# Row loads after the mixture of experts split over three queues, and attention outputs copied by ScalarE alone

## The reference

```python
for i in range(2):
    h += mixer_i(rmsnorm(h))        # layer 0: latent attention with a paged cache; layer 1: chunked gMLP gating
    h += hier_moe(rmsnorm(h))       # 4 groups x 8 experts, the 2 best of one group per token
    h += sigmoid(rmsnorm(h) @ ple_w_gate) * (p_i @ ple_w_proj)
y = rmsnorm(h)

# the end of the attention
o = einsum('bshc,chv->bshv', o_lat, w_uv)      # 8 heads, 256 latent -> 128
mix = o.reshape(...) @ w_o

# hier_moe: gates is zero except at the token's two experts
a = silu(t @ w_gate[e]) * (t @ w_up[e]) * gates[:, e]
y = sum over e of a @ w_down[e]
```

## Time and profile before

| | us |
|---|---|
| runs shown | 1202.03, 1206.19, 1210.29 |
| profiled execution, its own time | 1208.84 |
| its span | 1207.1 |
| PE busy | 1090.9 (90% of the span) |
| DVE busy | 362.3 (30%) |
| ACT busy | 194.0 (16%) |
| POOL busy | 115.3 (10%) |
| chain that ended last | PE 67%, DMA 22%, DVE 4%, issue 3% |
| row loads, POOL's queue | 8 of 512 KB (median 6.0 us from issue to landing), 4 of 128 KB (6.9 us) |
| weight stream, SP's queue | 250 of 1024 KB (18.7 us) |

### The profile page before, as it was taken

How to read it: one execution, slowest core, us unless ns; L and a number is a source line. 1 busy time by engine, 2 the same in 40 slices (tenths; PEclk the granted TensorE clock), 3 DMA queues, 4 the chain that set the end, 5 groups by cost and what they waited for, 6 DMA issues and landing times.

```text
span 1207.1 us, 14547 instructions
## 1 busy us (share of the span) xinstructions
PE 1090.9 (90%) x5302; PEld 667.0 (55%) x5302; DVE 362.3 (30%) x909; ACT 194.0 (16%) x398; POOL 115.3 (10%) x152
## 2 busy tenths in 40 slices
PE   5898879999998888899999999999999998887793
PEld 4675547644443333577777777777654443332372
DVE  1233432432221211353225544420332222210164
ACT  2121211311111111222111211000121111111121
POOL 0124200011111110100000000000011111110101
PEclk9898989989999999999999999999989999999996
DMA  9727727269999999783333433334349999999521
GB/s 384 263 75 225 224 90 309 79 250 403 419 419 419 419 419 376 304 361 110 135 128 117 140 105 105 105 128 139 108 155 396 419 417 418 419 419 422 204 102 40
DMA packets 62597, 306.81 MB, mean 254 GB/s; under 512 B 13730, under 2 KB 23170, under 8 KB 30402
## 3 DMA queue, kind: packets, MB, share of 16 engines
q1 hardware_dynamic: 45936, 276.52, 58.1%
q0 software_dynamic: 13632, 22.58, 5.8%
q10 hardware_dynamic: 2962, 6.80, 1.5%
HBM read 308.88 MB, written 21.08 MB: 273 GB/s over the span
## 4 chain that ended last, share of the span: by engine, by line
PE 67%; DMA 22%; DVE 4%; issue 3%; ACT 1%; SPq 0%; ACTq 0%; POOL 0%; POOLq 0%; DVEq 0%
DMA ring_sb<-stream 22%; PE ps L1558 16%; PE ps L1413 11%; PE ps L1606 8%; PE ps L1422 4%; PE ps L1491 3%; PE ps L1328 3%; PE ps L1143 2%; PE ps L1163 2%; PE ps L1371 2%; PE ps L1131 2%; PE ps L1362 1%; PE ps L1509 1%; PE ps L1507 1%; PE ps L1236 1%
## 5 line engine op out<-in xcount | busy, mean ns | idle before, releaser
L1413 PE MATMUL ps<-ring_sb,scr_sb 128*64 128x512 f32 x1024 | 238.3, 613 | 39.4 <-DMA ring_sb<-stream 39.4
L1558 PE MATMUL ps<-hn_sb,ring_sb 128*128 128x288 f32 x768 | 195.0, 408 | 0.0
L1413 PEld LDWEIGHTS ps<-ring_sb,scr_sb 128*64 128x64 f32 x1024 | 79.3, 140 | 193.2 <-issue 193.1
L1558 PEld LDWEIGHTS ps<-hn_sb,ring_sb 128*128 128x128 f32 x768 | 142.6, 190 | 37.3 <-DVE hn_sb L715 0.3
L1422 PE MATMUL ps<-ring_sb,scr_sb 128*64 128x512 f32 x512 | 123.7, 628 | 2.1 <-ACT scr_sb L602 1.9
L950 DVE SCALAR_TENSOR_TENSOR scr_sb<-ps,scr_sb 128x256 f32<-128x256 f32 x32 | 15.5, 484 | 266.9 <-ACT scr_sb L598 266.9
L1606 PE MATMUL ps<-scr_sb,ring_sb 128*128 128x288 f32 x384 | 95.3, 407 | 0.0
L1606 PEld LDWEIGHTS ps<-scr_sb,ring_sb 128*128 128x128 f32 x384 | 72.2, 190 | 19.4
L1422 PEld LDWEIGHTS ps<-ring_sb,scr_sb 128*64 128x64 f32 x512 | 35.5, 142 | 63.7 <-issue 60.0
L1491 PE MATMUL ps<-scr_sb,ring_sb 128*128 128x288 f32 x256 | 64.3, 406 | 0.0
L345 POOL DMA_INDIRECT scr_sb<-hn_rows,scr_sb x32 | 32.5, 1017 | 299.9 <-DVE scr_sb L927 275.1
(11 more groups left out here) (251 smaller groups left out, 1119.0 us busy)
## 6 DMA issues: line engine op xcount, KB each, us to landing
ring_sb<-stream SPq DMA_DIRECT2D x250, 1024.0 KB, 18.7
scr_sb<-key_pages SPq DMA_DIRECT2D x64, 192.0 KB, 3.4
ring_sb<-row_pages POOLq DMA_DIRECT2D x64, 128.0 KB, 3.2
scr_sb<-y_rows POOLq DMA_DIRECT2D x8, 512.0 KB, 6.0
hn_rows<-scr_sb ACTq DMA_DIRECT2D x4, 512.0 KB, 3.8
h_sb<-x SPq DMA_DIRECT2D x1, 1152.0 KB, 5.5
scr_sb<-bs ACTq DMA_DIRECT2D x1, 640.0 KB, 13.4
scr_sb<-p ACTq DMA_DIRECT2D x2, 288.0 KB, 5.2
```

What stands on the lines that cost most here:

```text
L1413: last = mm(ps[64 * a:64 * a + 64, 2 + b, :], xT[:, k, 64 * a:64 * a + 64], slot(a + 2 * (k // 4))[:, (k % 4) * 512:(k % 4) * 512 + 512], ...
L1558: last = mm(bank((i + 1) % 4, T), ring(s, (i % 2) * D + k * P, P), hn_t[:, k, :], start=(k == 0), stop=(k == KD - 1))
```

## The change

Two edits. The six row loads are shared out by token tile: tile 0 by SP, tile 1 by ACT, tile 2 by POOL. POOL raises a new semaphore `rows_put` where it used to issue all six; SP and ACT wait for it. SP's two loads stand just ahead of the waits that it had already. ACT's two stand behind its branch and ahead of its table load. And all eight heads are copied by ACT, with one semaphore `o_sb` in place of `o_a` and `o_d`; DVE only waits for the last head's matmuls.

```diff
+    def load_rows(engine, L, t):
+        t0, tn = TOK[t]
+        for k in range(2):
+            engine.dma_start(y12[0:tn, k, t, :], y_rows[L][k * T + t0:k * T + t0 + tn, :]
+                             ).then_inc(sem(f"y12_in{t}"), 16)
...
             if s == S_GATE[0]:
+                sp.wait_ge(sem("rows_put"), 1)
+                load_rows(sp, 0, 0)
                 sp.wait_ge(sem("y12_in1"), 32)
                 sp.wait_ge(sem("y12_in2"), 32)
...
             if s == S_GATE[1]:
+                sp.wait_ge(sem("rows_put"), 2)
+                load_rows(sp, 1, 0)
                 sp.wait_ge(sem("y12_in1"), 64)
                 sp.wait_ge(sem("y12_in2"), 64)
...
-            for t, (t0, tn) in enumerate(TOK):
-                for k in range(2):
-                    pool.dma_start(y12[0:tn, k, t, :], y_rows[L][k * T + t0:k * T + t0 + tn, :]
-                                   ).then_inc(sem(f"y12_in{t}"), 16)
+            pool.sem_inc(sem("rows_put"), 1)
+            load_rows(pool, L, 2)
...
-        for h in range(0, H, 2):
+        for h in range(H):
             act.wait_ge(sem("o_ps"), h + 1)
-            nc.scalar.activation(oT[:, h, :], bank(h % 4, T), ACT.Copy).then_inc(sem("o_a"), 1)
+            nc.scalar.activation(oT[:, h, :], bank(h % 4, T), ACT.Copy).then_inc(sem("o_sb"), 1)
...
+            act.wait_ge(sem("rows_put"), L + 1)
+            load_rows(act, L, 1)
             nc.scalar.activation(eps[:, 2:3], eps[:, 0:1], ACT.Sqrt)
...
-        for h in range(1, H, 2):
-            dve.wait_ge(sem("o_ps"), h + 1)
-            nc.vector.tensor_copy(oT[:, h, :], bank(h % 4, T)).then_inc(sem("o_d"), 1)
+        dve.wait_ge(sem("o_ps"), H)
...
-                pe.wait_ge(sem("o_a" if h % 2 == 0 else "o_d"), (h - 4) // 2 + 1)
+                pe.wait_ge(sem("o_sb"), h - 3)
...
-        pe.wait_ge(sem("o_a"), H // 2)
-        pe.wait_ge(sem("o_d"), H // 2)
+        pe.wait_ge(sem("o_sb"), H)
```

## The result

The changed kernel took 1210.6 us (median of 20 runs, 1204.53 to 1219.3); the kernel before, beside it, 1204.15 us. The ratio is 1.0045, 95% interval 1.0027 to 1.0063: **0.45% slower, 5.4 us by the ratio**. The medians themselves lie 6.5 us apart. The forecast was 0.26% slower, 1209.3 us. The sign, the place and the mechanism were right, the size came out larger.

The account below looks back on a forecast made before the run. PE and what it waits for were taken to bound the kernel. Late tile 1 rows (1.6 + 1.5 us) less 0.05 for the last head copy gave 1206.2 + 3.1 = 1209.3 us; range (1206 - 3) to 1216.

Parts of the forecast that it names:

- What bounds it; the margins: Before the combination: PE sets the end, without waiting for row loads, which land 1.6 and 1.3 us ahead of it.
- Tile 0 to SP, tile 2 on POOL: nothing: Row loads of tiles 0 and 2: both hidden, tile 0 in 6 us ahead of PE; cost and gain 0.
- Tile 1: time of issue: ACT's row loads, behind its last copy and branch: first issue at 495.11 in layer 0, 1140.47 in layer 1.
- Rival 1: Nothing is late: ACT's sequencer runs ahead and issues from 494.2; 0.1 us a layer, 1206.4 us; chance 0.22.
- Tile 1: time to land: ACT's row loads: 4.9 and 4.8 us from first issue, so 1.6 and 1.5 us late for PE's combination.
- What is late next: First gate slot and spatial weights after the combination: slot's margin 0.5 to 0.6 us, weights' 1.4 us; taken at 0.
- ACT's table load and first square: ACT behind its two row-load issues: table load ends at 497.3, covered by the first square at about 501.9; 0.
- The head copies: All eight on ACT: it keeps up, only the last copy is on the path, a gain of 0.05 us.
- Rival 2: PE's clock falls at the combination or an ACT issue is slow: up to 1216.8 us; chance 0.13.
- Rival 3: Faster: row loads before the change land later in other executions, so PE waits; 1.1 us at most, 1205.1; chance 0.05.
- The sum: Whole kernel: 1.6 + 1.5 - 0.05 = +3.1 us, 1209.3 us on the median, 0.26% slower.
- The promise of the change: Parallel issue of the six row loads: POOL's issues take 3.19 us, their landing is hidden, so no gain.

Follow-up runs that it names:

- the kernel with one filler: The kernel before with 1 keep-busy matmul instead of 3 in front of the combination: 1207.39 us, ratio 1.0017.
- the kernel with four large loads on SP: The changed kernel with tile 1 loaded by SP behind tile 0, instead of by ACT: 1209.17 us, ratio 1.0016.
- the rows alone: The changed kernel with the head copies given back to DVE, so only the row loads moved: 1211.27 us, ratio 1.0058.

## Why the prediction was right, and where its size was off

- **What bounds it; the margins.** Right for the trace that it read: PE did not wait, and the margins were 1.6 and 1.3 us, as the kernel with one filler shows. For every execution it is too strong: the prediction took over PE's arrival behind a down product at half clock, and in layer 1 of the kernel with only the head copies, at full clock, PE waited 1.04 us for rows issued by POOL.
- **Tile 0 to SP, tile 2 on POOL: nothing.** Right. SP's loads were in long before, and the kernel with four large loads on SP has no gap.
- **Tile 1: time of issue.** Right. From the end of PE's last down product to ACT's first issue: 1.07 us forecast and 1.08 measured in layer 0 (498.07 to 499.15), 0.84 forecast and 0.86 in layer 1. Rival 1, a sequencer that runs ahead, did not happen.
- **Tile 1: time to land.** The mis-sized term. Forecast 4.9 and 4.8 us, from a slot of the same bytes on idle queues; measured 5.7 and 7.0 (5.8 and 6.7, 5.8 and 7.7, 5.8 and 6.9 in the three other traces with the same loads). So the gaps were 2.5 and 3.9 us and not 1.6 and 1.5. Both lie inside the bound named, 8.0 us. The row taken was the nearest in bytes, but not in its surroundings: in these traces transfers of instructions run on the DMA engines beside the load, and in layer 1 its last part comes late on one to three of them. Without the branch the landings were 4.8 and 5.3 us, one run.
- **What is late next.** Right. The first gate slot landed 4.8 us behind its issue in both layers, and in layer 0 PE takes it up at 510.58 without a gap, 5.6 us behind its first combination.
- **ACT's table load and first square.** Right: hidden.
- **The head copies.** Right: the last copy hands over 0.1 us sooner, not measurable in the time.
- **Rival 2.** It came in part: in two of the three traces with the full late load and three fillers the clock fell in or behind the gap of layer 1 (3.86 and 4.45 us), in one it didn't (3.57 us). A fall cost 3.1 and 3.7 us of combination, about twice the 1.8 us priced, since it lasted through five or six of its steps. In layer 0 of these three, with 2.5 to 2.6 us, it never fell. In the kernel without the branch it fell behind shorter gaps, 1.94 us in layer 0 and 2.36 us in layer 1 (there the gap in front of the fillers is shorter too, 1.02 and 0.83 us), so a gap's length alone doesn't decide it.
- **Rival 3.** Its condition is real: in the kernel with only the head copies the rows of layer 1 landed 0.85 us behind the end of PE's fillers (1143.67 against 1142.82). A kernel before that waits at times loses less by the change than the sum says.
- **The sum.** By the traces it should be 2.6 + 4.0, and some 2 us for a fall in two of three: 8 to 9 us. The ratios say 5.4, 4.7 and 7.0 us for the changed kernel, its repeat and the rows alone. Part of the rest is that the kernel before waits too in some executions: from the end of the last down product to the combination of layer 1 its own trace has 4.15 us, the kernel with only the head copies 5.2, the traces with the full late load 7.6 to 8.6. The stream-bound stretch ahead of it gives nothing back that can be told: from the first gate-up product to the start of the last matmul of the down product of layer 1 243.2 to 246.3 us pass in the kernels with the late load, 243.5 to 246.4 in the others, and 1.7 us of these spreads is the clock of the last down product. What makes up the remainder is open. So there is luck in the number: with the gaps as measured the sum is 6.6 us, above the +1 to +6 that the prediction gave its forecast, and that the 5.4 us lie inside it isn't owed to the estimate of the landing.
- **The promise of the change**, rows that come sooner by parallel issue, had nothing to give: all the issuing was under PE's last pair. The Trainium skill's rule (DMA: Bandwidth & Descriptors, "Issuing engines are not separate DMA queues"), that only issuing time is saved, agrees with the traces here: POOL's 3.19 us shrank to 1.09 us and nothing followed.
- The Trainium skill's fit (DMA: Bandwidth & Descriptors, "Anatomy of one DMA": about 2.0 us plus bytes over 436 GB/s, an estimate of 4.4 us for 1 MB) is made for a DMA issued by GpSimd. For ACT's two loads it is below every measured landing, 4.8 to 7.7 us; here the measurement decides.

Open: why the kernel with ACT's loads ahead of its last copy is 0.3% faster than before, twice. From the start of the last matmul of the down product to the combination its two traces have 4.8 and 4.5, 4.8 and 4.6 us, the trace of before 4.8 and 4.6; the kernel with only the head copies has 4.8 and 5.8. So where the down product runs at full clock it saves the 1 us that POOL's loads then cost (in its second trace, layer 1: rows in at 1138.41, PE at 1138.80 without a gap). At most some 2 us of the 3 to 4 can come from there. Its mean granted clock over the runs is 0.969 and 0.968 against 0.967, which would be worth 1 to 3 us at most; what keeps the clock up isn't shown. It is open too why tile 1 on SP, equally without a gap in its trace, came out at 1.0016 and this kernel at 0.9967: a difference of total times as large as the effect under study, for which no trace shows a cause. The gaps in the traces carry the argument, the total times alone wouldn't. A variant with the copies on DVE was not tried.

## What to carry to other kernels

A transfer moved to another engine's queue starts when that engine's order lets it, not when its data are ready: look up what stands ahead of it there and when that ends. Spreading loads over queues pays only if their issue is on the path; here a copy that ended 0.8 us after PE's last matmul put the issue of 1 MB of rows 7 us behind the moment at which they were ready. Estimate a landing from a row in like surroundings, not only of like size: just behind a branch, look for transfers of instructions on the same DMA engines. Read a margin from more than one execution: here PE's arrival alone moved it by 1.7 us. And filler matmuls under a wait are cheap; take them out only when the trace shows that the clock holds without them.

## What the runs showed of the hardware

- Transfers of instructions share the 16 DMA engines with data. One of them (16 KB, about 1 us) beside a load of 1 MB went with a landing at 5.7 to 5.8 us; two of them (16 and 8 KB) with a tail of 2.1 to 2.7 us on one to three engines and a landing at 6.7 to 7.7 us, four traces each; without any it was 4.8 and 5.3 us, one run. Beside a load of 512 KB two of them made no tail (4.0 us, one trace).
- Whether a gap costs the clock isn't told by its length: gaps of 2.5 to 2.6 us (three traces) and of 3.6 us did not, gaps of 1.9, 2.4, 3.9 and 4.5 us did, each behind 2.8 us of solid matmuls.
- The last down product took 5.35 us with the granted clock at 0.50 over a part of it, and 3.65 us with it at 1.00 throughout. By itself that moves PE's arrival by 1.7 us, more than the margin of the kernel before (1.6 and 1.3 us).
- Ahead of any changed instruction the executions differ by up to 10 us: the first head matmul started between 173.6 and 183.2 us over the traces. Two single traces can't be subtracted from end to end.
